# Four pairs of projections as seven Strassen products each, and a double-buffered token mixing beside them

## The reference

```python
(na_q, na_k, na_v, na_gate, pool_u, pool_gate, rw_r, rw_k, rw_v, rw_gate,
 rw_lw, rw_la, merge_logits) = jnp.split(h @ w_in, IN_SPLIT_POINTS, axis=-1)
...
r, k, v = (z + m * (centred_neighbour_mean(z) - z)
           for z, m in ((r0, mu[0]), (k0, mu[1]), (v0, mu[2])))
kk = to_heads(k * k_k, RWKV_HEADS)
kk = kk / jnp.maximum(jnp.sqrt(jnp.sum(kk * kk, axis=-1, keepdims=True)), 1e-12)
```

## Time and profile before

| | |
|---|---|
| median of three runs | 3966.21 us |
| profiled execution, span | 3972.9 us |
| TensorE busy, share | 3748.5 us, 94% |
| VectorE busy, share | 1423.5 us, 36% |
| ScalarE, GpSimd | 668.7 and 556.5 us |
| gemm_hq, TensorE's matmuls | 512, 220.0 us busy |
| granted TensorE clock by slices | 0.9 or more in all but one of 40 |
| DMA, mean | 201 GB/s |

### The profile page before, as it was taken

How to read it: one execution, slowest core, us unless ns; L and a number is a source line. 1 busy time by engine, 2 the same in 40 slices (tenths; PEclk the granted TensorE clock), 3 DMA queues, 4 the chain that set the end, 5 groups by cost and what they waited for, 6 DMA issues and landing times. The chain is left out here.

```text
span 3972.9 us, 59313 instructions
## 1 busy us (share of the span) xinstructions
PE 3748.5 (94%) x25117; PEld 1884.2 (47%) x25117; DVE 1423.5 (36%) x2605; ACT 668.7 (17%) x1327; POOL 556.5 (14%) x797
## 2 busy tenths in 40 slices
PE   8799998999999999999999999998998889899998
PEld 1354443334544444554444444453346667665443
DVE  0399993352322214321100023445533334341411
ACT  0100001122211100331100000135532222221000
POOL 0011110121000001000000011441212333321100
PEclk9899999999999999999999999999999999999999
DMA  8778995982255556335555488638863333334762
GB/s 298 286 287 297 363 375 190 326 315 82 69 201 170 180 174 235 105 131 188 176 181 168 145 310 294 229 117 294 273 203 115 107 120 106 101 98 165 245 210 97
DMA packets 355527, 797.43 MB, mean 201 GB/s; under 512 B 26334, under 2 KB 62198, under 8 KB 350394
## 3 DMA queue, kind: packets, MB, share of 16 engines
q1 hardware_dynamic: 255696, 459.69, 34.7%
q0 software_dynamic: 72304, 272.53, 19.1%
q10 hardware_dynamic: 27266, 61.45, 4.0%
HBM read 685.37 MB, written 108.22 MB: 200 GB/s over the span
## 5 line engine op out<-in xcount | busy, mean ns | idle before, releaser
L1139 PE MATMUL gemm_a_g_ps<-store_w,turned 128*128 128x512 f32 (+1 forms) x1152 | 455.1, 557 | 2.4 <-PEq L205 2.4
L1139 PE MATMUL out_c_g_ps<-store_w,turned 128*128 128x512 f32 (+1 forms) x1024 | 399.3, 552 | 0.0
L839 DVE SCALAR_TENSOR_TENSOR pmods_acc<-pmods_w,cond,pmods_acc 128x512 f32<-128x512 f32 x540 | 384.3, 748 | 25.5 <-DMA pmods_w<-in_w_mod 1.3
L1139 PEld LDWEIGHTS gemm_a_g_ps<-store_w,turned 128*128 128x128 f32 x1152 | 208.4, 190 | 248.5 <-issue 248.5
L2532 PE MATMUL scan_g_ps<-store_w,turned 64*64 64x512 f32 x2048 | 292.5, 613 | 21.6 <-issue 14.0
L1139 PEld LDWEIGHTS out_c_g_ps<-store_w,turned 128*128 128x128 f32 x1024 | 184.5, 190 | 213.8 <-issue 213.8
L1139 PE MATMUL att_a_g_ps<-store_w,turned 128*128 128x512 f32 x512 | 240.2, 599 | 7.0 <-ACT outlet_stage L2280 4.2
L1139 PE MATMUL gemm_hq_g_ps<-store_w,turned 128*128 128x512 f32 x512 | 220.0, 592 | 1.7 <-PEq L3363 1.7
L1139 PE MATMUL out_a_g_ps<-store_w,turned 128*128 128x512 f32 x512 | 220.6, 592 | 0.9 <-ACT turned L1499 0.9
L1139 PE MATMUL out_a_g_ps<-store_w,turned_c 128*128 128x512 f32 x512 | 220.2, 592 | 0.0
L1139 PE MATMUL feat_g_ps<-store_w,turned 128*128 128x512 f32 x384 | 182.4, 624 | 14.6 <-ACT outlet_stage L1815 12.4
(11 more groups left out here) (441 smaller groups left out, 4795.4 us busy)
## 6 DMA issues: line engine op xcount, KB each, us to landing
store_w<-in_w_in SPq DMA_DIRECT2D x160, 1024.0 KB, 5.7
pmods_w<-in_w_mod POOLq DMA_DIRECT2D x40, 2048.0 KB, 12.7
store_w<-in_a_w_in SPq DMA_DIRECT2D x48, 1024.0 KB, 12.5
store_w<-in_c_w_in SPq DMA_DIRECT2D x48, 1024.0 KB, 5.1
mods_w<-in_w_mod SPq DMA_DIRECT2D x32, 1024.0 KB, 9.4
store_w<-in_a_w_out SPq DMA_DIRECT2D x32, 1024.0 KB, 5.0
scan_raw<-s_feat SPq DMA_DIRECT2D x112, 256.0 KB, 4.9
s_feat<-feat_o POOLq DMA_DIRECT2D x16, 1536.0 KB, 7.6
```

Of the source, the lines that this page charges most:

```text
L839: v.scalar_tensor_tensor(a, src, x, a, ALU.mult, ALU.add)
L1139: mm = pe.matmul(to, lhs, self.store.slot[i % self.store.NS][:, k, :width], start=first, stop=last)
```

## The change

Two neighbouring chunks of 512 columns make a pair. With the depth halved (8 depth tiles each: 0 and 1), the two token tiles and the two chunks give a 2x2 by 2x2 block product, and the change computes it with the seven products of Strassen's scheme (in Winograd's form) in the order 1, 5, 6, 3, 7, 2, 4. Each is 8 depth tiles of 128x128 by 128x512, accumulated in one PSUM bank.

- VectorE makes the sums of inputs once, in token tiles 2 and 3 of `turned` (`PairInputs`), and per pair four weight forms of 8 depth tiles by 512 columns, each in four pieces (`make_form`). Forms 1, 2 and 4 use a new buffer, form 3 is written over the quarters of the block w01.
- ScalarE copies products 1 and 5 out of PSUM; VectorE makes the seven sums u2, u4, y01, u3, y11, y00, y10 in the output buffers; ScalarE issues the four stores.
- `Store` counts pairs: 8 quarters per pair in the order w00, w01, w11, w10; each waits for the product that last reads the quarter six before it and for the form made from it. `Ring.claims` gives every product its bank.
- The mixing has two sets of buffers. GpSimd issues the loads of tiles 0 and 1 and the vectors at once, makes the sums of neighbours (10 adds of 128x1024 that VectorE made before), then finishes tile 0, loads tile 2, finishes tile 1, loads tile 3, makes the sums of tiles 2 and 3, and finishes them. VectorE's part is cut into 46 steps, one instruction each but for the last of a tile; `project_pairs` puts 4 of them into the first pair's list and 14 into each other's, at fixed places.

```diff
+        def gpsimd_program(pool):
+            def average(n):
+                pool.wait_ge(loaded[n % 2], 16 * (9 if n < 2 else 15))
+                for j in used(n):
+                    pool.tensor_tensor(z[n % 2][j][:, 1, :], z[n % 2][j][:, 1, :], z[n % 2][j][:, 2, :], ALU.add).then_inc(averaged, 1)
+            def finish(n):
+                rows = slice(n * P, (n + 1) * P)
+                pool.wait_ge(squared, n + 1)
+                pool.tensor_tensor(stat[:, 1, :], stat[:, 0, :], half[:, :], ALU.pow).then_inc(rooted, 1)
+                pool.wait_ge(done, n + 1)
+                return all_dma(pool, [(mixed[j, rows, :], z[n % 2][j][:, 0, :]) for j in ((0, 1, 2) if n < 2 else (1,))]
+                               + [(mixed[3, rows, :], kk[n % 2][:, :])]
+                               + [(feat[d, F_V, rows, :], z[n % 2][2][:, 0, :]) for d in range(2)], stored[n % 2])
...
+            load(0)
+            all_dma(pool, [(vec[:, j, :], a.partition_broadcast(P)) for j, a in enumerate(
+                (I["rw_mu_2"][0, 0], I["rw_mu_2"][0, 1], I["rw_mu_2"][0, 2], I["rw_k_k_2"][0]))], vec_loaded)
+            load(1)
+            average(0)
+            average(1)
+            for n in range(2):
+                count = finish(n)
+                pool.wait_ge(stored[n], count)
+                load(n + 2)
+            average(2)
+            average(3)
+            for n in range(2, 4):
+                count = finish(n)
+                pool.wait_ge(stored[n % 2], 96 + count)
+
+        def vector_steps(v):
+            v.wait_ge(vec_loaded, 64)
+            averages = 0
             for n in range(4):
+                zn, kn = z[n % 2], kk[n % 2]
+                for j in used(n):
+                    averages += 1
+                    v.wait_ge(averaged, averages)
+                    v.scalar_tensor_tensor(zn[j][:, 1, :], zn[j][:, 1, :], 0.5, zn[j][:, 0, :], ALU.mult, ALU.subtract)
                     v.drain()
+                    yield
+                    v.tensor_tensor(zn[j][:, 1, :], zn[j][:, 1, :], vec[:, j, :], ALU.mult)
                     v.drain()
+                    yield
+                    v.tensor_tensor(zn[j][:, 0, :], zn[j][:, 0, :], zn[j][:, 1, :], ALU.add)
                     v.drain()
+                    yield
...
+PAIR_ORDER = (1, 5, 6, 3, 7, 2, 4)
+PAIR_LOADS = ((0, 0), (0, 1), (1, 0), (1, 1), (1, 2), (1, 3), (0, 2), (0, 3))
...
+    def pair_units(self, pe, n, wait_tile_taken):
...
+        for product in PAIR_ORDER:
+            wait_ready(pe, product)
+            for j in range(len(low)):
+                self.wait_bank(pe, (product, n, j), wait_tile_taken)
+            for piece in range(store.pieces(m)):
+                half = piece // per_half
+                if product in (1, 3, 2):
+                    i = load + {1: 0, 3: 4, 2: 6}[product] + half
+                    store.wait_quarter(pe, i)
+                    src = store.quarter(i)
+                else:
+                    pe.wait_ge(store.piece_made, store.made_count(m, {5: 1, 6: 2, 7: 3, 4: 4}[product], piece))
...
+    def make_form(self, v, n, form):
...
+            if form == 1:
+                store.wait_quarter(v, load + half)
+                store.wait_quarter(v, load + 2 + half)
+                if earlier:
+                    old = self.base + earlier[-1]
+                    same = store.pieces(old) == store.pieces(m)
+                    v.wait_ge(store.piece_read, store.read_count(old, 4, piece if same else store.pieces(old) - 1))
+                v.tensor_tensor(made, w01, w00, ALU.subtract).then_inc(store.piece_made, 1)
+            elif form == 2:
+                store.wait_quarter(v, load + 4 + half)
+                v.wait_ge(store.piece_read, store.read_count(m, 5, piece))
+                v.wait_ge(store.piece_made, store.made_count(m, 1, piece))
+                v.tensor_tensor(made, w11, made, ALU.subtract).then_inc(store.piece_made, 1)
+            elif form == 3:
+                v.tensor_tensor(w01, w11, w01, ALU.subtract).then_inc(store.piece_made, 1)
+            else:
+                store.wait_quarter(v, load + 6 + half)
+                v.wait_ge(store.piece_read, store.read_count(m, 6, piece))
+                v.tensor_tensor(made, w10, made, ALU.subtract).then_inc(store.piece_made, 1)
...
+        @block.vector
+        def _(v):
+            rest = side_steps(v)
...
+            for n in range(len(g.jobs)):
...
+                if n == 0:
+                    inputs.make(v, 0)
+                for _piece in g.make_form(v, n, 1):
+                    pass
+                if n:
+                    beside(3)
+                if n == 0:
+                    inputs.make(v, 1)
+                for _piece in g.make_form(v, n, 2):
+                    pass
+                if n == 0:
+                    inputs.make(v, 2)
+                    inputs.make(v, 3)
+                for _piece in g.make_form(v, n, 3):
+                    pass
+                outlet.wait_free(v, o + 3)
+                g.sum_u2(v, n, 0, stage[0], stage[3])
+                outlet.wait_free(v, o + 2)
+                g.sum_u4(v, n, 0, stage[3], stage[1], stage[2])
+                for _piece in g.make_form(v, n, 4):
+                    pass
+                g.sum_y01(v, n, 0, stage[2])
+                if n:
+                    beside(3)
+                g.sum_u3(v, n, 0, stage[3])
+                g.sum_y11(v, n, 0, stage[3], stage[1])
+                if n:
+                    beside(4)
+                g.sum_y00(v, n, 0, stage[0])
+                beside(4)
+                g.sum_y10(v, n, 0, stage[3])
...
-        h_rest = h_chunks(LAT, H_NQ, H_NG) + h_chunks(LAT, H_PU, H_PG)
+        def in_pairs(chunks):
+            return [((a[0], b[0]), tuple((tb,) for tb in a[1]), a[2], (a[3], b[3])) for a, b in zip(chunks[::2], chunks[1::2])]
+        h_rest = in_pairs(h_chunks(LAT, H_NQ, H_NG) + h_chunks(LAT, H_PU, H_PG))
...
-        project(nc, "gemm_hq", store, outlet, xt(512), h_rest, rwkv_mix(nc, "rmix", proj_h, I, rw, outlet))
+        h_inputs = PairInputs(nc, "h_inputs", turned[:, :], turned[:, :], KD, 512, (0,), (1,), (2,), (3,))
+        project_pairs(nc, "gemm_hq", store, outlet, h_inputs, h_rest, rwkv_mix(nc, "rmix", proj_h, I, rw, outlet))
```

More of the change, by code:

```diff
@@ new lines, in load @@
+    def load(self, sp, end):
+        for i in range(self.issued, min(end, len(self.loads))):
+            n, q = self.loads[i]
+            if self.pair[n]:
+                side, q = PAIR_LOADS[q]
+                src = self.jobs[n][0][side].rearrange("(k p) n -> p k n", p=P)
+            else:
+                src = self.jobs[n][0].rearrange("(k p) n -> p k n" if self.jobs[n][1] != 1 else "(p k) n -> p k n", p=P)
+            kq = src.shape[1] // 4
+            if i >= self.NS:
+                self.wait_freed(sp, i - self.NS)
@@ new lines, in __init__, with claim_banks @@
+        self.n_adds = [sum(7 * len(job[1][0]) for job, p in zip(jobs[:n], self.pair) if p) for n in range(len(jobs))]
+    def claim_banks(self):
+        self.claims = []
+        for n, job in enumerate(self.jobs):
+            if self.pair[n]:
+                self.claims += [(product, n, j) for product in PAIR_ORDER for j in range(len(job[1][0]))]
+            else:
+                self.claims += [("tile", n, j) for j in range(len(job[1]))]
+        self.claim_of = {who: m for m, who in enumerate(self.claims)}
@@ new lines, in project_pairs, with _, beside @@
+def project_pairs(nc, name, store, outlet, inputs, projections, side, n_banks=8):
+    with ExitStack() as st:
+        g = Ring(nc, st, f"{name}_g", store, [(w, tbs, inputs.tile, inputs.wait) for w, tbs, func, dst in projections], n_banks)
+        out_of = outlet.take(4 * len(projections))
+        copied = nc.alloc_semaphore(f"{name}_copied")
+        side_steps, gpsimd_program = side(st)
+        block = st.enter_context(nc.Block(no_gpsimd_drain=True))
+        block.gpsimd(gpsimd_program)
+        @block.sync
+        def _(sp):
+            g.load_all(sp)
+        @block.tensor
+        def _(pe):
+            for n in range(len(g.jobs)):
+                g.multiply_pair(pe, n)
+        @block.vector
+        def _(v):
+            rest = side_steps(v)
+            def beside(count):
+                for _step in range(count):
+                    next(rest, None)
+            for n in range(len(g.jobs)):
+                o = out_of + 4 * n
+                stage = [outlet.stage[(o + x) % 4][:, :] for x in range(4)]
+                if n == 0:
[18 more added lines that the diff above has]
+                for _piece in g.make_form(v, n, 4):
+                    pass
+                g.sum_y01(v, n, 0, stage[2])
[8 more added lines that the diff above has]
+                g.sum_y10(v, n, 0, stage[3])
+            for _step in rest:
+                pass
+        @block.scalar
+        def _(act):
+            for n, (w, (low, high), func, dst) in enumerate(projections):
```

(7 more changed lines are left out.)

257 lines of the change are left out of this document (200 added, 57 removed).

## The result

The changed kernel takes 3988.99 us (median of 4 runs, 3986.90 to 3992.59) where the kernel before takes 3967.78 on the same chip (4 runs): a ratio of 1.0062, 95% interval 1.0048 to 1.0076, so slower by 0.6%. The forecast was 3968 us with a range of 3951 to 3981; the time lies above it.

The account below looks back on a forecast made before the run. TensorE was taken as the bound, busy 3748.5 of 3972.9 us. A wait and a store tail eat the 27.5 us saved: next stage +0.6, half clock +1.7, emptier queues -0.7, sum +1.6 on 3966.2, so 3968 us, range 3951 to 3981.

Parts of the forecast that it names:

- The work removed: TensorE in the changed stage: seven block products replace eight, 448 matmuls instead of 512, 27.5 us less work.
- what bounds the stage after: VectorE works in one written order in which TensorE waits for its forms, 177 us of work in 192.
- the gap: TensorE before form 1 of pair 3: waits 15.2 us from t = 151, released by VectorE's form.
- the clock's fall: TensorE after its long idle time: granted clock at 0.50, 1.7 us lost on the first 32 matmuls.
- the add's duration: GpSimd's add of 128x1024: 2.35 us by the slope, at most 2.55.
- the tail of stores: Stage end: tile 3's stores take 8.6 us after the last step, barrier 0.5; next stage at t = 222.1.
- VectorE and GpSimd slow each other: Rival: VectorE's passes slow down beside GpSimd's averages, +11 to +13 us, 3979 us; chance 0.10.
- The wait itself: VectorE at t = 138 waits 17.9 us (bounds 14.5 to 18.1) for GpSimd's average of tile 2.
- the 12.4 us from the rescaling to tile 3's first load: GpSimd's interval measured in the kernel before, taken over as a term: 12.4 + 3.15 + 2.35 = 17.9 us.
- The loads' cover of 1.6 us: Pair 1's third quarter lands at t = 52, needed by 53.8; loads cost nothing, at most 5 us.
- 0.3 us of small waits: TensorE in pair 1: product 7 ends at 82.8, with 0.3 us of small waits included.

Follow-up runs that it names:

- x2_order: Changed kernel with GpSimd's sums of tile 2 moved ahead of its finish of tile 1: 3963.63 us, ratio 0.9997 to the kernel before.
- x9_mixonly: Kernel before, keeping its plain product, with the changed kernel's token mixing and queue order: 3965.35 us, ratio 0.9991 to the kernel before.
- x1_tiny: Changed kernel with GpSimd's ten sums of neighbours cut to 16 of 1024 columns: 3980.02 us, ratio 1.0043 to the kernel before.
- x8_kinds: Kernel before with spare GpSimd adds, copies and memsets beside VectorE's mixing, and one-operand VectorE passes in tile 3: 3984.26 us in one execution.
- x5_sched: Changed kernel with each tile's sums right behind its load and the 46 mixing steps placed anew: 3953.95 us, ratio 0.9967 to the kernel before.
- x7_ordertiny: Changed kernel with tile 2's sums ahead of tile 1's finish and all GpSimd sums cut to 16 columns: 3960.73 us, ratio 0.9984 to the kernel before.
- b_again: Kernel before, unchanged, profiled once more on the chip of the other runs: 3964.81 us, span 3963.0 us, stage 221.55 us.

## Why the prediction was wrong

**Right.** The work removed, 448 matmuls; what bounds the stage after (VectorE's written order); the place, the releaser and the kind of the gap; the clock's fall and its price of 1.7 us; the add's duration (2.34 for 2.35 us); that the tail of stores ends the stage and the next one starts half-clocked. x2_order and x9_mixonly show the mechanism: taken away by moving the sums, harmless where no form stands behind.

**The step that failed is "VectorE and GpSimd slow each other", put down as a rival with a chance of 0.10 and left out of the sum at nothing.** It was worth some 8 of the 17.6 us by which the next stage is late (2.2 before tile 1's end, 5.8 behind the wait, by x1_tiny); I had sized it at 11 to 13 us and argued it away. The argument had two parts. The row was of a pass that reads PSUM, and I said so; such a pass is indeed untouched (0.69 us at 2471.78, in the midst of the doubled ones). The other part was the prediction's inference from two pages of the Trainium skill, that only a two-port mode blocks and tensor_tensor has none. x8_kinds shows that a plain two-operand pass waits too. The Trainium skill (SBUF — State Buffer, "SBUF: two separate sides") says so: the port pair is locked for a whole instruction by a VectorE operation in a two-port mode, or by one with two SBUF inputs against a GpSimd operation that reads SBUF. The traces agree in every kind tried: add 3.20, copy 1.90, memset 1.23 us for the pass. In the ledger this is the +5.6 behind the wait and about half of the +4.3 before it: form 1 of pair 1, four pieces in 4.62 us alone, took 7.89.

**The wait itself was undersized: 22.96 us for 17.9, outside its bounds of 14.5 to 18.1.** The term at fault is the 12.4 us from the rescaling to tile 3's first load, read off before, and its upper bound, which took it as given. Behind it lies, as these traces read, the load of the queues. They stood so while tile 1's six stores landed (packets, megabytes, share of 16 engines), the kernel before, from 2421.0 to 2433.5:
```profile
q0 software_dynamic: 864, 3.15, 66.5%
q1 hardware_dynamic: 793, 1.59, 35.4%
```
and the kernel after, from 2444.4 to 2461.6:
```profile
q1 hardware_dynamic: 1699, 3.35, 51.3%
q0 software_dynamic: 864, 3.15, 44.7%
```
The stores are the same 3.15 MB; the weights (q1) moved 1.59 MB in 12.5 us before and 3.35 MB in 17.2 us after, 379 and 380 GB/s in all. The pair's first six quarters are asked for in a burst when the last pair's slots come free, and tile 1's stores fell into it. In x5_sched, where tile 1's and tile 0's are issued 32 us earlier (t = 111 for 143, t = 64 for 96), 1.35 and 0.94 MB of weights went beside them, and GpSimd waited 10.50 and 9.44 us instead of 13.90 and 15.36. That the burst sets the wait is read from these traces; no run changed the burst alone. Nor does it take a burst: in x9_mixonly, with the product of the kernel before, the same six stores kept GpSimd waiting 16.04 us, with 3.20 MB of weights and 1.35 MB of tile 2's loads beside them. What the traces have in common is how much else was moved.

**The loads' cover of 1.6 us was mostly used up.** The quarter for form 1 of pair 1 was forecast for t = 52, 3.2 us after VectorE could have started, and had to be there by 53.8. It came at t = 53.2, after VectorE had waited 4.17 us, and TensorE waited 0.51 us for the first piece. Of the +4.3 at tile 1's end this and the meetings share; x1_tiny has tile 1 done 2.2 us earlier (2441.81 for 2444.10, from starts 0.1 us apart), so the meetings are about half of it. The other half is a gap of TensorE of 2.10 us before form 2 of pair 1 that stays in x1_tiny, where the forecast had 0.3 us of small waits.

**The tail** took 12.3 us for 9.1, by the traces for the same reason as the wait: I took its stores as alone, but the next stage's weights, released when product 4 ended at 2526.3, were in flight beside them. In x2_order, where the product had ended 8 us before the last step, it took 8.4. The weights' queue from the last step to the next stage, in the kernel after and in x2_order:
```profile
q1 hardware_dynamic: 988, 1.95, 43.0%
...
q1 hardware_dynamic: 86, 0.15, 4.8%
```
x7_ordertiny has after's distance (2.5 us from the product's end to the last step), after's 1.95 MB and after's tail (12.6 us). No run changed these weights alone.

**The median.** The stage is 18.1 us longer than in b_again, the next one 1.8, and the medians 21.2: the 1.3 us left are part of what b_again left open. I had noted that the profiled execution of before lay 6.7 us above the median and worked in differences, which was right; read as spans, 3989.2 against 3972.9, the loss would look like 16.3.

## What to carry to other kernels

When an engine that others wait for gets a second job, write down for every instruction in front of theirs what it waits for on the other queue, and order that other queue by who waits, not by tile: one `average` moved ahead of a store wait was worth 25.9 us of the stage. Work handed from VectorE to GpSimd is off VectorE only in time in which VectorE's passes over SBUF don't meet it; here ten adds of 2.3 us cost as much as ten passes of 1.3 us. And put the last step of side work a store's landing time before the last matmul: the 12 us between the stages of x2_order and x5_sched come from that.

## What the runs showed of the hardware

- A VectorE pass over SBUF that starts beside a GpSimd add waits out the rest of the add: 3.20 us for 1.23 (two operands), 2.68 for 0.69 (copy or scaling of one). Then GpSimd's next add waits for VectorE's pass (3.32 us for 2.34, the second add of the row at 2471.86 in the kernel after). A pass that reads PSUM (0.69) and passes beside a GpSimd memset (1.23) are untouched. The one-operand case was not expected; it was the dearest by ratio, 3.9 times.
- Six stores of 0.52 MB kept GpSimd waiting 8.9 us (before) to 16.3 us (x7_ordertiny) behind the last issue, with 1.59 and 4.31 MB of weights moved beside them; all queues together made 379 GB/s (before) to 412 GB/s (x9_mixonly) in such stretches where they had work throughout.
- Two executions of the unchanged kernel differ by 10.4 us in one part, from 1439.1 to 1449.5 us, at the same code, so a gain of 8 us in one stage can't be read off two spans.
